# Each scatter-add of a mixture-of-experts block issued as two transfers of 64 quarter rows

## What is computed

```python
def expert_block(args):
    xb, e = args
    return (jax.nn.silu(xb @ w_g[e]) * (xb @ w_u[e])) @ w_d[e]

out = lax.map(expert_block, (buf.reshape(n_blocks, EXPERT_BLOCK, D), block_eid)).reshape(n_rows, D)
y = jnp.sum(out[slot_dest].reshape(n_tok, TOP_K, D) * gates[..., None].astype(h.dtype), axis=1)
return y.reshape(B, S, D)
```

## Time and profile before

| | us |
|---|---|
| median of 3 runs | 2784.62 |
| lowest, highest | 2781.67, 2787.75 |
| span of the profiled execution | 2769.6 |
| PE busy in it | 2604.3 (94%) |
| POOL busy in it | 805.8 (29%) |
| expert stage in it, from the first gather to the last add | 1921.8 to 2761.6 |

### The profile page before, as it was taken

One profiled execution on the slowest core, in us unless ns is written; L12 is line 12 of the kernel. 1 busy time (PEld: TensorE's weight loads), 2 busy tenths in 40 slices (PEclk: granted clock), 3 DMA queues, 4 the chain that ended last, 5 costly groups with the idle time before them and its releaser, 6 DMA issues. The chain is left out here.

```text
span 2769.6 us, 87168 instructions
## 1 busy us (share of the span) xinstructions
PE 2604.3 (94%) x37008; PEld 1718.1 (62%) x37009; DVE 1176.3 (42%) x2440; ACT 904.4 (33%) x1687; POOL 805.8 (29%) x916
## 2 busy tenths in 40 slices
PE   8999999999999998788888889996999999999998
PEld 3444444444477776677777745554776777777775
DVE  2333321212499998576666623335222222222222
ACT  1111110000377777666666533442111111111111
POOL 0000040000000000766666411112444444444444
PEclk9999999999999999899999999997999999999999
DMA  4111141111212221111112036531998997989893
GB/s 141 57 57 57 57 126 46 68 45 68 77 34 78 74 72 49 31 49 47 39 49 58 15 117 212 194 118 60 298 298 260 306 297 248 298 261 340 282 300 60
DMA packets 241149, 370.01 MB, mean 134 GB/s; under 512 B 35009, under 2 KB 134849, under 8 KB 238242
## 3 DMA queue, kind: packets, MB, share of 16 engines
q1 hardware_dynamic: 213186, 328.72, 34.6%
q0 software_dynamic: 27744, 38.03, 6.6%
HBM read 296.17 MB, written 70.52 MB: 132 GB/s over the span
## 5 line engine op out<-in xcount | busy, mean ns | idle before, releaser
L2343 PE MATMUL gu_ps<-gate_up_,xT 128*32 128x256 f32 x6336 | 425.0, 381 | 9.0 <-DVE h L2426 1.0
L2343 PEld LDWEIGHTS gu_ps<-gate_up_,xT 128*32 128x32 f32 x6336 | 274.1, 109 | 127.2 <-issue 65.4
L347 PE MATMUL ps<-low,high 128*128 128x512 f32 x768 | 337.6, 596 | 2.4 <-issue 2.4
L2412 DVE STREAM_TRANSPOSE xT<-xg 128x256 f32<-128x256 f32 x145 | 94.8, 654 | 517.0 <-PE gu_ps L2343 513.5
L2352 PE MATMUL y_ps<-down_,hT 128*32 128x256 f32 x4608 | 313.6, 379 | 0.6 <-ACT y L2391 0.6
L2303 POOL DMA_INDIRECT xg<-h,take x146 | 144.7, 991 | 425.0 <-DVE h L2426 403.3
L2352 PEld LDWEIGHTS y_ps<-down_,hT 128*32 128x32 f32 x4608 | 225.4, 110 | 46.2 <-ACT y L2391 1.1
L347 PEld LDWEIGHTS ps<-low,high 128*128 128x128 f32 x768 | 144.6, 192 | 173.4 <-issue 173.4
L2311 POOL DMA_INDIRECT out<-y,put x144 | 227.0, 1577 | 60.1 <-issue 55.2
L722 DVE TENSOR_TENSOR_SCAN h_all<-h_all 128x512 f32<-128x512 f32 x192 | 239.0, 1304 | 2.8 <-ACT h_all L680 2.3
L1782 PE MATMUL ps<-high 128*128 128x512 f32 x512 | 231.7, 603 | 7.1 <-DMA high<-mixT 7.1
(11 more groups left out here) (326 smaller groups left out, 4319.0 us busy)
## 6 DMA issues: line engine op xcount, KB each, us to landing
down_<-in_w_exp_down SPq DMA_DIRECT2D x128, 512.0 KB
gate_up_<-in_w_exp_gate SPq DMA_DIRECT2D x88, 512.0 KB
gate_up_<-in_w_exp_up SPq DMA_DIRECT2D x88, 512.0 KB
high<-in_w_exp_gate SPq DMA_DIRECT2D x40, 512.0 KB
high<-in_w_exp_up SPq DMA_DIRECT2D x40, 512.0 KB
pT<-low SPq DMA_DIRECT2D x13, 1024.0 KB, 3.9
rkv<-pT SPq DMA_DIRECT2D x96, 128.0 KB, 2.5
high<-in_x SPq DMA_DIRECT2D x16, 512.0 KB, 4.0
```

Source lines behind the costliest of these rows:

```text
L347: done = pe.matmul(qkv_ps[:, part, :], hT[:, s, k, :], w_sb[:, k, part * SBW:(part + 1) * SBW], start=(k == 0), stop=(k == KT - 1))
L2343: last = pe.matmul(gu_ps[QUARTERS[q], 0:2 * P].rearrange("t (x f) -> t x f", x=2), xT[:, k * ROWS:(k + 1) * ROWS], w_gu[s][:, k, :, q * P: ...
L2412: dve.transpose(xT[:, :].rearrange("p (k t) -> p k t", k=KT), xg[j][:, :].rearrange("t (p k) -> t k p", k=KT))
```

## The change

`put[j]` is no longer 128 numbers in a column but 64 in each of two columns. DVE fills them with two copies in place of one, and the second raises `rows_known`. POOL issues two indirect adds of 64 quarter rows (partitions 0 to 63, that is quarters 0 and 1 of the 32 tokens, then partitions 64 to 127), the second directly behind the first without a wait of its own. Each raises `stored[j]` by 16, so everyone who waits for `stored[j]` now waits for multiples of 32. Nothing else changes.

```diff
+        HALVES = [slice(0, P // 2), slice(P // 2, P)]
...
-        put = [sb(f"put7{j}", [P, 1], I32) for j in range(2)]
+        put = [sb(f"put7{j}", [P // 2, 2], I32) for j in range(2)]
...
-                def add(b, j):
+                def add_half(j, half):
+                    rows = HALVES[half]
+                    pool.indirect_dma_start(out=out_quarters[:, :], out_offset=bass.IndirectOffsetOnAxis(ap=put[j][:, half:half + 1], axis=0),
+                                            in_=y[j][rows, :], in_offset=None, compute_op=ALU.add).then_inc(stored[j], 16)
+
+                def add_first(b, j):
                     pool.wait_ge(rows_known, b + 3)
                     pool.sem_inc(on_pool, 1)
                     pool.wait_ge(y_copied, b + CREDIT + 1)
                     pool.sem_inc(on_pool, 1)
-                    pool.indirect_dma_start(out=out_quarters[:, :], out_offset=bass.IndirectOffsetOnAxis(ap=put[j][:, 0:1], axis=0),
-                                            in_=y[j][:, :], in_offset=None, compute_op=ALU.add).then_inc(stored[j], 16)
+                    add_half(j, 0)
...
                     gather(j)
-                    add(b, j)
+                    add_first(b, j)
+                    add_half(j, 1)
...
                 for j in range(2):
-                    add(last * 2 + j, j)
+                    add_first(last * 2 + j, j)
+                    add_half(j, 1)
...
-                    pool.wait_ge(stored[j], last * 16 + 16)
+                    pool.wait_ge(stored[j], last * 32 + 32)
...
-                        act.wait_ge(stored[j], i * 16)
+                        act.wait_ge(stored[j], i * 32)
...
-                        dve.wait_ge(stored[j], i * 16)
-                    dve.tensor_copy(put[j][:, :], to_all[:, bass.ds(b, 1)]).then_inc(rows_known, 1)
+                        dve.wait_ge(stored[j], i * 32)
+                    dve.tensor_copy(put[j][:, 0:1], to_all[HALVES[0], bass.ds(b, 1)])
+                    dve.tensor_copy(put[j][:, 1:2], to_all[HALVES[1], bass.ds(b, 1)]).then_inc(rows_known, 1)
```

## The result

The kernel with two halves took 2886.17 us (median of 4 runs, 2883.76 to 2887.68), the kernel before 2783.57 beside it (4 runs, 2781.67 to 2787.75): 1.0363 times as long, 95% interval 1.0348 to 1.0378. The forecast was 2785.7 us and no change that can be measured; the kernel became 3.6% slower, some 103 us.

The account below looks back on a forecast made before the run. The prediction took PE to bound the expert stage. 144 blocks x 0 on PE and +1.1 us at the end, added to the 2784.6 us median, gave 2785.7 us, range 2780 to 2793.

Parts of the forecast that it names:

- So this stage is bound by PE: Expert stage: PE busy 98.6 to 98.8 us of every 100, blocks every 5.75 us, all other engines wait for it.
- 144 blocks x 0 on PE: Expert stage: the second add lies in POOL's idle time, so each block costs PE 0.
- rival 4: Expert stage, faster: earlier landings or other gaps between weight loads gain something, 2772 or 2778 us; chance 4%.
- signs of being wrong: c above 1.5, xT over 0.70 us, y copy's wait ended by POOL or landing, gathers not following h by 0.8.
- c: POOL's time for one 64-row indirect add: taken as 1.2 us, bounds 0.79 and 1.58.
- Landing: Adds' rows reaching memory: 0 to 1.1 us later, but never last for ACT's y copy; 0 on the path.
- rival 1: DVE's short path, slower: POOL's second half stretches xT, hT and h by 0.1 us a block, 2800; chance 8%.
- rival 2: Expert stage, slower: POOL's cycle or late landings become the bound, 2870 or 2856 us; chance 3%.
- The end: Program end, POOL on the path: last add ends 1.56 us later, less 0.5 for landing, +1.1; ends -0.2 and +5.8.
- the 0.5 that I took off: Program end: the last landing shortened by 0.5 us because only 64 rows are left for the DMA engines.
- the two-halves rule: Program end: transfers on two partition halves serialize, each half taking as long as the whole; +1.6 instead of +1.1.
- The drain: POOL's final drain, 5.45 us before: if it went by transfers issued (290 before, 434 now), it would add 2.7.

Follow-up runs that it names:

- after_b: The changed kernel (two 64-row adds a block) word for word, one run: 2703.58 us beside 2702.00 for the kernel before.
- group 1: The first measurement, runs made side by side: kernel before 2783.57 us, changed kernel 2886.17 us.
- group 9: Runs made side by side: kernel before 2773.63 us, one 64-row add a block 2753.64, one add of 128 half rows per two blocks 2703.91.
- group 3: Runs made side by side: kernel before 2775.38 us, changed kernel again 2860.9, kernel with three adds a block (64, 32, 32 rows) 2889.45.
- first_half_only_b: The changed kernel with its first 64-row add alone, the other 64 rows never added: 2753.64 us beside 2773.63 for the kernel before.
- after_again: The changed kernel word for word, two runs: 2860.9 us beside 2775.38 for the kernel before, ratio 1.0312.
- add_or_scatter: The kernel before with scatter-adds in even blocks and overwriting scatters in odd blocks: 2775.72 us beside 2776.82 for the kernel before.
- half_rows_pairs: The kernel before with one scatter-add of 128 half rows (2 KB) per two blocks, 72 in all: 2706.61 us beside 2705.05; repeated, 2703.91 beside 2773.63.
- x_no_adds: The kernel before without any scatter-add, POOL raising the semaphore itself: 2697.25 us beside 2702.71 for the kernel before.
- no_adds_b: The kernel before without any scatter-add, run again word for word: 2694.37 us beside 2702.00 for the kernel before.
- groups with holes: Sets of side-by-side runs where the kernel before took 2771 to 2788 us; holes are stretches without a weight load that no semaphore explains.
- groups without: Sets of side-by-side runs where the kernel before took 2698 to 2711 us, without the unexplained stops in PE's weight loads.

## Why the prediction was wrong

**The bound.** "So this stage is bound by PE" was right, but the step from there, that whatever lies beside PE's work is hidden, was not. PE's 98.8% is a modelled number that hides late weight loads: 96 loads and matmuls take 5.2 us in after_b and took 5.75 us before. Over 0.5 us in each block was lost already and looked like work.

**The step that failed** is the sum's first term, "144 blocks x 0 on PE", and behind it rival 4, which read the 0.4 us of issue in the earlier trace rows as at most something to gain, and from DMA traffic at large. It bounded that gain by the idle time of PE in the earlier trace rows (9.0 and 3.7 us), whose ends are modelled, and not by that of the weight loads. The hole stood 0.4 to 0.75 us behind the start of the scatter-add at 2206.08, in the row under it, and there were 217 of them, 95.3 us in all. Doubling the adds took them to 425 and 197.3 us, and a block from 5.75 to 6.49 us. What they cost by the runs: one add of 128 rows (2783.57 - 2702) / 144 = 0.57 us a block in group 1 and (2773.63 - 2702) / 144 = 0.50 in group 9, one of 64 rows (2753.64 - 2702) / 144 = 0.36 in group 9, two of 64 rows (2886.17 - 2702) / 144 = 1.28 in group 1 and 1.10 in group 3. (2702 is the level without holes, from other groups, so these are rough to some 0.1.) Two halves cost more than twice one half; why was not tried. Part of it may be that `gate_up` then waits for `h`: 68 times in the kernel after, 2 times in first_half_only_b.

None of the signs of being wrong that the prediction named came (c over 1.5, a longer xT, a copy ended by another than PE), except that 4 of some 140 gathers started more than 1 us behind `h`. They looked at POOL, DVE and the landings; what moved was the time from block to block.

**c, the 64-row add on POOL.** Taken 1.2 us, bounds 0.79 and 1.58, measured 1.42. The argument that what is dearer in an add than in a gather goes by rows was wrong: 128, 64 and 32 rows take 1.58, 1.42 and 1.32. The plain scatter at 0.99 shows that the 0.59 belong to the addition. The error in c cost nothing in the stage: the gap of 0.30 was right, and POOL kept 2.1 us of idle time ahead of 120 of the gathers.

**Landing.** Right: each of the 144 copies of y is still ended by PE.

**DVE (rival 1).** False. The copies took 0.10 and 0.15 us, together 0.14 more than before, and the medians of xT, hT and h are 654, 422 and 336 ns, as before within 2 ns, though the second half now lies beside other work. The Trainium skill ("SBUF — State Buffer", section "Who interferes with whom") has DVE and GpSimd block each other only where the DVE instruction is in a mode that uses two ports or has two inputs in SBUF, a condition that the prediction left out. No run shows whether these instructions meet it, so their unchanged times are no test of the rule.

**POOL as the bound (rival 2).** Its time, 2856 to 2870, came nearest, but by another mechanism: POOL's waits for h say that it is not the bound. That the number came near is luck. POOL is the bound with three transfers.

**The end.** Forecast +1.1, ends -0.2 and +5.8. In order of time, POOL alone:

```profile
2868.47 1.41 POOL L2309 DMA_INDIRECT out<-y,put  x1 [3.14 <-DVE put L2425]
...
2873.61 1.41 POOL L2309 DMA_INDIRECT out<-y,put  x1 [0.30 <-DMA out<-y,put]
...
L2341 POOLq EVENT_SEMAPHORE  x2: 17/17/17, 2873.3 to 2876.7; - x2
...
L2342 POOLq DRAIN  x1: 7045/7045/7045, 2876.8 to 2876.8; - x1
```

From the start of the last but one block's add to the end of the last add it is 6.55 us, before 4.14: +2.4 for a forecast of +1.6, by c. The landing takes 1.7 us where it took 2.2: the 0.5 that I took off was right. It is so in after_again and after_b too (1.8 us each). The prediction had worked out from the two-halves rule of the Trainium skill ("SBUF — State Buffer", section "Can I just issue two DMAs to hit both halves?") that a half would land no sooner than the whole; these three landings don't bear that out. The drain takes 7.05 us for 5.45, +1.6. Together +3.5, inside the bounds. The drain does not go by the transfers, as I had set it out as a possibility: it takes 2.84 us without adds, 3.74 with add_or_scatter, 4.55 with one 64-row add a block, 5.78 with plain scatters, 6.51 with half_rows_pairs, 7.42 with three adds. Kernels that were profiled more than once had the same drain to the nanosecond each time.

**Was the sum right where there are no holes?** after_b took 1.6 us more than before, the sum was +1.1. One run each can't show more than that the change is within some 13 us of nothing; but 103 us is excluded. There the prediction's 0 on PE holds, so what it lacked in the stage is the hole beside each add.

**What stays open.** How a scatter of 1 KB rows holds up the weight loads is not shown, nor why it does so in one group of runs and not in the other. The kernel without any scatter (x_no_adds, no_adds_b) never ran in a group with holes, so the plainest test, holes gone when the scatters are, is missing; that the holes belong to the scatters rests on their fixed distance from each start, on their doubling, and on the kernels of half rows. One regularity, which is no cause: the groups with holes (3, 6, 9, 10) all began with a kernel of 144 or more scatters, and the groups without (2, 4, 5, 7, 8) with a kernel of at most 72. That a kernel of half rows is free of holes rests on three runs of two kernels, in two groups in which the kernel before was on its slower level.

## What to carry to other kernels

On an engine that is 98% busy by a profile with modelled ends, count the records in a stretch and compare them with the best stretch that you know: a short idle time with no releaser, again and again at the same distance from another engine's transfer, may be a price that this transfer already costs, and one that doubles with the transfers. When you split a scatter-add, its time on POOL hardly falls (1.58 to 1.42 us for half the rows). The kernels with wider rows (2 KB for 1 KB) moved as many bytes with half the rows and had none of the holes; and measure on more than one group of runs, since here the same kernel stood 3% apart from itself.

## What the runs showed of the hardware

- In the traces of groups 1, 3, 6 and 9, weight loads of PE nearly stop twice beside a scatter of 1 KB rows into HBM, add or not, the second time from 0.8 or 0.9 to 1.3 or 1.4 us behind its start; not beside a gather, and not in groups 2, 4, 5, 7 and 8. The first packet of an add's rows starts 2.18 us or more behind the add's start (add_or_scatter, 72 adds).
- The same kernel before took 2698 to 2711 us in five groups and 2771 to 2788 in five, at the same clock; chips 9 and 13 showed both.
- POOL's time for an indirect DMA: gather of 128 rows 0.99 us, plain scatter of 128 rows 0.99, scatter-add of 128, 64 and 32 rows 1.58 to 1.63, 1.42 to 1.44, 1.32 to 1.33; of 128 and 64 rows of 2 KB 1.62 and 1.44. The next one starts 0.30 us behind it.
- POOL's drain at the end takes 2.84 to 7.42 us, by the program and the same each time, with no simple relation to the number of transfers.
- From the end of the last add on POOL to the start of the drain pass 1.8 to 1.9 us when it has 64 quarter rows (five traces) and 2.3 when it has 128 (before, one trace).
